# Prompt attention by pairs of heads, with transposed probabilities multiplied into transposed outputs

## What is computed

```python
q = rms_norm((h @ w_q).reshape(B, T, 16, 64), q_norm)
for each block of 128 queries, over keys up to its end:
    s = einsum('bqhd,bkhd->bhqk', q, k) * 64 ** -0.5
    s = s + f_query - f_key          # running sums of log forget gates
    s = where(key <= query, s, -1e30)
    p = softmax(s)
    o = einsum('bhqk,bkhd->bqhd', p, v)
y = concat(o) @ w_o
```

## Time and profile before

| | us |
|---|---|
| median of 3 runs | 1319.04 |
| lowest and highest | 1318.5, 1324.37 |
| the profiled execution, its own time | 1321.06 |
| its span, first to last instruction | 1319.4 |
| PE busy in the span | 1120.7 |
| DVE, ACT, POOL busy | 449.5, 254.2, 131.6 |

### The profile page before, as it was taken

One profiled execution on the slowest core, in us unless ns is written; L12 is line 12 of the kernel. 1 busy time (PEld: TensorE's weight loads), 2 busy tenths in 40 slices (PEclk: granted clock), 3 DMA queues, 4 the chain that ended last, 5 costly groups with the idle time before them and its releaser, 6 DMA issues.

```text
span 1319.4 us, 18188 instructions
## 1 busy us (share of the span) xinstructions
PE 1120.7 (85%) x6958; PEld 633.6 (48%) x6958; DVE 449.5 (34%) x1065; ACT 254.2 (19%) x580; POOL 131.6 (10%) x228
## 2 busy tenths in 40 slices
PE   3996799999997399999977888769966999999980
PEld 0553444444554244445546767545444544445540
DVE  3555601111111540642166676321366011101115
ACT  2232011111111311111123444211120111111111
POOL 4100100000000200000112000210000000000003
PEclk9897799999999699999998999889987999999995
DMA  9998799999999568633424000845034899999976
GB/s 354 380 396 337 256 365 412 413 414 401 400 387 391 201 255 291 260 133 112 150 65 116 0 0 0 245 96 188 16 136 168 326 414 411 411 401 398 387 301 211
DMA packets 66301, 349.55 MB, mean 265 GB/s; under 512 B 6873, under 2 KB 8449, under 8 KB 53378
## 3 DMA queue, kind: packets, MB, share of 16 engines
q1 hardware_dynamic: 46944, 289.72, 56.0%
q0 software_dynamic: 15360, 52.91, 12.7%
q10 hardware_dynamic: 3938, 6.09, 1.3%
HBM read 325.44 MB, written 27.20 MB: 267 GB/s over the span
## 4 chain that ended last, share of the span: by engine, by line
PE 67%; DMA 12%; DVE 11%; issue 5%; ACT 2%; ACTq 2%; POOL 1%; SPq 0%; DVEq 0%; POOLq 0%
PE pb L1151 15%; PE pb L918 11%; PE pb L908 11%; PE pb L954 5%; PE pb L962 5%; DMA h<-h_d,idx 4%; DMA ring<-in_ada_w_dram 3%; PE pb L779 3%; PE pb L1253 2%; PE pb L901 2%; DMA hT_raw<-f_d 2%; PE pb L826 2%; DVE ring L2346 1%; PE pb L1230 1%; PE pb L1102 1%
## 5 line engine op out<-in xcount | busy, mean ns | idle before, releaser
L1151 PE MATMUL pb<-ring,hT_raw 128*128 128x512 f32 x512 | 231.4, 607 | 3.7 <-DVE ring L2207 1.9
L918 PE MATMUL pb<-ring,h 128*64 128x256 f32 (+1 forms) x2176 | 186.5, 345 | 0.0
L1151 PEld LDWEIGHTS pb<-ring,hT_raw 128*128 128x128 f32 x512 | 97.3, 194 | 122.8 <-issue 122.1
L908 PE MATMUL pb<-ring,h 128*128 128x512 f32 x320 | 147.9, 613 | 2.0 <-DVE h L2027 2.0
L918 PEld LDWEIGHTS pb<-ring,h 128*64 128x64 f32 (+1 forms) x2176 | 116.5, 127 | 61.1 <-issue 15.6
L2114 DVE COPY hT_raw<-pb 64x512 f32<-64x512 f32 (+1 forms) x26 | 18.0, 693 | 253.5 <-PE pb L962 146.8
L908 PEld LDWEIGHTS pb<-ring,h 128*128 128x128 f32 x320 | 60.6, 197 | 72.0 <-issue 72.0
L779 PE MATMUL pb<-ring,cT 128*32 128x512 f32 (+1 forms) x576 | 60.1, 556 | 26.2 <-DMA ring<-in_ada_w_dram 26.2
L962 PE MATMUL pb<-ring,hT_raw 128*64 128x512 f32 x352 | 80.1, 597 | 1.0 <-issue 1.0
L954 PE MATMUL pb<-ring,hT_raw 128*128 128x512 f32 x160 | 71.3, 599 | 0.0
L671 POOL DMA_DIRECT2D ys_d<-hT_raw x32 | 18.0, 564 | 489.0 <-DVE hT_raw L2114 397.3
(11 more groups left out here) (333 smaller groups left out, 1329.2 us busy)
## 6 DMA issues: line engine op xcount, KB each, us to landing
ring<-in_w_down_dram SPq DMA_DIRECT2D x32, 2048.0 KB, 14.0
ring<-in_w_gate_dram SPq DMA_DIRECT2D x32, 2048.0 KB, 11.5
ring<-in_w_up_dram SPq DMA_DIRECT2D x32, 2048.0 KB, 12.9
ring<-in_ada_w_dram SPq DMA_DIRECT2D x24, 2048.0 KB, 10.1
ring<-in_kv_ada_w_dram SPq DMA_DIRECT2D x4, 2048.0 KB, 10.0
ring<-in_w_kvf_dram SPq DMA_DIRECT2D x4, 2048.0 KB, 18.5
ys_d<-hT_raw POOLq DMA_DIRECT2D x10, 512.0 KB, 7.8
h_d<-h ACTq DMA_DIRECT2D x8, 512.0 KB, 7.4
```

What stands on the lines that cost most here:

```text
L908: last = T.matmul(bank[:, :], xgT[:, par, k, :], w[:, k * DE:(k + 1) * DE], start=(k == 0), stop=(k == KC - 1))
L918: last = T.matmul(bank[n * a:n * a + n, c0:c0 + cols], xgT[:, par, k, t0:t0 + n], w[:, k * DE + cols * a:k * DE + cols * a + cols], start= ...
L1151: last = T.matmul(bank[:, :], hT[:, k, col[t]:col[t] + P], w[:, k * 512:(k + 1) * 512], start=(k == 0), stop=(k == KC - 1))
```

## The change

The loop is written out, without registers, as 32 steps m: eight pairs times four query tiles in the order 0, 3, 1, 2, each step with both heads of the pair.

- Scores: the masks go first into two PSUM banks, one per head; then each head's product runs on its own 64 rows of the array (`tile_position=(64 * s, 0)`), both heads in turn, with `qT` itself as the weights. `qz` and its copies go: the scale of the scores is multiplied into the query norm's gain once.
- The bias is read from `nfb` in place; POOL's copies go. POOL multiplies the probabilities by the inverse sums instead (`at_sc`), 128 x w per head and step, ahead of the transposes.
- Transposed tiles are copied so that tiles 0 and 1, and tiles 2 and 3, lie side by side (`PTa`, `PTb`). DVE copies tiles 0, 1 and 2, ACT tile 3. The value product has a 64-column block of values as the weights and up to 256 columns of transposed probabilities moving; head s writes rows 64 s to 64 s + 63 of a bank. So outputs come out transposed, two halves a pair, and ACT copies them to `oT`.
- The output projection reads `oT`; only the sample tile is still transposed, from `oo_s`. The output weights are loaded with rows in plain order.
- DVE prepares the sample group's queries after its second add instead of before the loop; DVE, not POOL, waits for the bias loads. The output weights' load waits for the last add, `load_values(1)` for the last scores, behind POOL's own steps.
- Layer 1's first expert loads go out as down, up, gate; up now waits for the end of the output projection too, as `oT` lies in its slot.

```diff
+    TURNS = (0, 3, 1, 2)
...
+    READY = [max(TURNS.index(2 * a), TURNS.index(2 * a + 1)) for a in range(2)]
...
-    o_v = w_o[0].rearrange("(p k) n -> p k n", k=KC)
+    o_v = w_o[0].rearrange("(k p) n -> p k n", p=P)
...
-                    elif kind == "g":
+                    elif kind != "d":
                         sp.wait_ge(o_done, 2 * NT)
...
-                for kind in (("d", "g", "u"), ("u", "d", "g"))[layer]:
+                for kind in (("d", "g", "u"), ("d", "u", "g"))[layer]:
...
-            sp.wait_ge(at_o, TP * NH + 1)
+            sp.wait_ge(at_add, 2 * STEPS)
...
+            for m in range(STEPS):
+                b = TURNS[m % TP]
                 for s in range(2):
-                    pool.wait_ge(at_add, 2 * TP * j + TP * (s - 1))
-                    g.tensor_copy(nfh[:, s, :], nfb[:, bass.ds(2 * j + s, 1), :, :].rearrange(
-                        "p o t k -> p (o t k)")).then_inc(at_nf, 1)
-            pool.wait_ge(at_o, TP * NH + 1)
+                    pool.wait_ge(at_rinv, m + 1)
+                    g.tensor_scalar(Sq[b][s], Sq[b][s], rs[:, 2 * b + s, 1:2], None, ALU.mult).then_inc(at_sc, 1)
+            pool.wait_ge(at_s, STEPS)
             load_values(1)
...
+            def masks(m):
+                if m >= 2:
+                    pe.wait_ge(at_add, 2 * m - 2)
+                b = TURNS[m % TP]
+                for s in range(2):
+                    last = T.matmul(pb[2 * (m % 2) + s][:, b * P:(b + 1) * P], identb[:, :], causal[:, :],
+                                    start=True, stop=False)
+                last.then_inc(at_c, 1)
+
+            def scores(m):
+                j, b = m // TP, TURNS[m % TP]
+                pe.wait_ge(at_c, m + 1)
+                for s in range(2 if b else 0):
+                    q = slice(HD * s, HD * s + HD)
+                    T.matmul(pb[2 * (m % 2) + s][:, 0:b * P], qT[q, j, b * P:(b + 1) * P], kT[q, j, 0:b * P],
+                             start=False, stop=False, tile_position=(HD * s, 0))
+                for s in range(2):
+                    q = slice(HD * s, HD * s + HD)
+                    last = T.matmul(pb[2 * (m % 2) + s][:, b * P:(b + 1) * P], qT[q, j, b * P:(b + 1) * P],
+                                    kT[q, j, b * P:(b + 1) * P], start=False, stop=True, tile_position=(HD * s, 0))
+                last.then_inc(at_s, 1)
+
+            def turn(m):
+                b = TURNS[m % TP]
+                pj, last_b = (m - 1) // TP, TURNS[(m - 1) % TP]
+                for s in range(2):
+                    pe.wait_ge(at_sc, 2 * m + s + 1)
+                    if m and last_b == TP - 1:
+                        pe.wait_ge(at_pa, 2 * pj + s + 1)
+                    elif m:
+                        pe.wait_ge(at_pt, 2 * (pj * (TP - 1) + DVE_TURNS.index(last_b)) + s + 1)
                     for c in range(b + 1):
+                        last = T.transpose(pb[4 + s][:, c * P:(c + 1) * P], Sq[b][s][:, c * P:(c + 1) * P], ident[:, :])
                     last.then_inc(at_t, 1)
...
+            def values(j, half):
...
+                for c in range(2 * half + 2):
+                    lone = c == 2 * half + 1
+                    for s in range(2):
...
+                        last = T.matmul(pb[6 + half][HD * s:HD * s + HD, (P if lone else 0):2 * P],
+                                        vv[:, c, (2 * j + s) * HD:(2 * j + s + 1) * HD], p,
+                                        start=(c == 0), stop=lone, tile_position=(0, HD * s))
+                last.then_inc(at_pv, 1)
...
+            for m in range(STEPS):
+                if m + 3 < STEPS:
+                    scores(m + 3)
+                turn(m)
+                for half in range(2):
+                    j, at = divmod(m - 1, TP)
+                    if m and at == READY[half]:
+                        values(j, half)
+                if m + 4 < STEPS:
+                    masks(m + 4)
+            values(NPAIR - 1, 1)
...
-            transposes(oo, 5, lambda t: pe.wait_ge(sa_o, 8) if t == TS else None, by_stride)
+            transposes(oo_s, 5, lambda t: pe.wait_ge(sa_o, 8), lambda src, t, k: src[:, k * P:(k + 1) * P], [TS])
...
+            def out(j, half):
+                act.wait_ge(at_pv, 2 * j + half + 1)
+                A.activation(oT[:, j, 2 * P * half:2 * P * half + 2 * P], pb[6 + half][:, 0:2 * P], ACT.Copy).then_inc(at_o, 1)
+
+            def copy_p(j):
+                if j:
+                    act.wait_ge(at_pv, 2 * j)
+                for s in range(2):
+                    act.wait_ge(at_t, 2 * (j * TP + TURNS.index(TP - 1)) + s + 1)
+                    A.activation(PTb[:, s, :, P:2 * P], pb[4 + s][:, :].rearrange("p (c t) -> p c t", c=TP),
+                                 ACT.Copy).then_inc(at_pa, 1)
...
+            for m in range(STEPS):
+                if m + 2 < STEPS:
+                    expo(m + 2)
+                for half in range(2):
+                    j, at = divmod(m - 2, TP)
+                    if m > 1 and at == READY[half]:
+                        out(j, half)
+                if TURNS[m % TP] == TP - 1:
+                    copy_p(m // TP)
...
+            def add(m):
+                j, b = m // TP, TURNS[m % TP]
+                w = (b + 1) * P
+                for s in range(2):
+                    if m >= TP:
+                        dve.wait_ge(at_t, 2 * (m - TP) + s + 1)
+                    dve.wait_ge(at_s, m + 1)
...
+                    V.tensor_tensor_reduce(out=Sq[b][s], in0=pb[2 * (m % 2) + s][:, 0:w], in1=bias, scale=1.0,
                                            scalar=-3e38, op0=ALU.add, op1=ALU.max,
...
+                dve.wait_ge(at_add, 2 * m + 2)
+                fq, top = Fs[:, b, 2 * j:2 * j + 2], mx[:, 2 * b:2 * b + 2, :]
+                tt(top[:, :, 1], top[:, :, 0], fq, ALU.add)
+                V.tensor_tensor(top[:, :, 2], fq, top[:, :, 1], ALU.subtract).then_inc(at_nb, 1)
...
+            dve.wait_ge(nfb_loaded, 2 * 16 * TP)
+            add(0)
+            add(1)
+            sample_queries()
+            inverse(0)
+            for m in range(STEPS):
+                if m + 2 < STEPS:
+                    add(m + 2)
+                if m + 1 < STEPS:
+                    inverse(m + 1)
+                if TURNS[m % TP] < TP - 1:
+                    copy_p(m)
```

More of the change, by code:

```diff
@@ L1245, in turn @@
                     last.then_inc(at_t, 1)
-                def values(n):
-                    s, b = divmod(n, TP)
-                    pe.wait_ge(at_pt, NB * j + n + 1)
-                    pe.wait_ge(at_o, NB * j + max(n, 1))
-                    for c in range(b + 1):
-                        last = T.matmul(pb[6 + n % 2][:, 0:HD], PT[:, n % 2, c * P:(c + 1) * P],
-                                        vv[:, c, bass.ds(j * 2 * HD + s * HD, HD)], start=(c == 0), stop=(c == b))
-                    last.then_inc(at_pv, 1)
@@ new lines, in _ @@
+            masks(0)
+            masks(1)
+            scores(0)
+            scores(1)
+            masks(2)
+            scores(2)
+            masks(3)
+            for m in range(STEPS):
[8 more added lines that the diff above has]
+                    masks(m + 4)
@@ new lines, in _ @@
+            expo(0)
+            expo(1)
+            for m in range(STEPS):
[7 more added lines that the diff above has]
+                    copy_p(m // TP)
+            for m in range(STEPS, STEPS + 2):
+                for half in range(2):
+                    j, at = divmod(m - 2, TP)
+                    if at == READY[half]:
+                        out(j, half)
```

194 lines of the change are left out of this document (73 added, 121 removed).

## The result

The changed kernel takes **1278.19 us** (median of 4 runs, 1275.87 to 1279.22), beside 1321.7 for the kernel before on the same chip: a ratio of 0.9647, 95% interval 0.9605 to 0.9689. The forecast of 1269 was 9 us too low, and 1278 lies inside its range. The profiled execution took 1279.22 us, its span is 1277.5.

The account below looks back on a forecast made before the run. The order of waits, not bytes or one full engine, was taken to bound prompt attention. Terms of -40 (stage), -5 (sample group) and -5 (transposed outputs) sum to -50 us: 1271 against the profile, 1269 as median; range 1255 to 1296.

Parts of the forecast that it names:

- The pair: Prompt attention loop: one pair of heads every 10.5 us, 9.75 from waits plus 0.75 for hops and collisions; bounds 9.3 and 13.2.
- POOL's price: POOL's eight multiplications by 1/sum in the loop: priced from its copy, up to twice that, 3.6 to 7.2 us a pair, hidden.
- The cover goes at about three times the copy's price: Loop: POOL's multiplications stay hidden beside DVE and ACT until they cost about three times its copy's 0.61 us at 512 columns.
- So ACT's order, not a full engine, sets 9.75: Loop: ACT's sequence of exponentials, last pair's output and tile 3's copies delays DVE and sets 9.75 us a pair.
- PE's 8.6: PE's work in the loop: values 2.2, scores 3.3, transposes 2.2 and masks 0.9 us, together 8.6 a pair.
- Rival 1: Loop on PE: halves don't overlap, or each tile shape change costs; 13.2 us a pair, 1288 us in all; chance 0.2.
- Rival 2: Loop: POOL and DVE hold each other off, slowing DVE's small operations; 13.2 us a pair, about 1288 us; chance 0.1.
- Rival 3: Loop: TensorE's clock stays at 1.2 GHz, PE takes 18.4 us a pair, slower at 1328 us; chance 0.06.
- The stage: Prompt attention up to the sample group's first transposes: ends at 785.0 instead of 824.9, 40 us less.
- Sample group: Group behind the loop: earlier weight and value loads, then its own arithmetic, save 5 us; bounds 2 and 7.
- Transposed outputs: Before the output projection: only the sample tile is still transposed, done in 1.7 us, saving 5 us.
- Layer 1's weights: Expert loads reordered to down, up, gate: later starts are covered by fifty us, so nil; otherwise the price of one load.

Follow-up runs that it names:

- e5: The changed kernel with POOL copying each score tile onto itself instead of multiplying it by 1/sum (division left out): 1267.03 us, ratio 0.9576.
- e1: The changed kernel without POOL's multiplications, PE's transposes waiting for the exponentials instead (probabilities left unnormalised): 1268.77 us, ratio 0.9585.
- e7: The changed kernel with ACT instead of POOL multiplying the second head of tiles 2 and 3, nothing left out: 1269.72 us, ratio 0.9588.
- e10: The changed kernel with POOL multiplying one head by constant 1.0, the other by a two-operand operation repeating the inverse-sum column: 1271.54 us, one run.
- e9: e7 with the next step's masks right behind the transposes, ahead of the value passes: 1267.18 us, ratio 0.9555.
- e3: The changed kernel with DVE instead of POOL multiplying tiles 0 and 1 by the inverse: 1277.4 us, ratio 0.964.

## Why the prediction was right, and where it was not

The sign, the size and most of the sum held. Against the forecast's -50 us the profiled span shrank by 41.9.

- **The pair** was forecast at 10.5 and is 10.13, but not for the reason given; that the numbers are close is in part luck, as the 0.75 us allowed for hops and collisions covered a price that the sum didn't have. The step that failed is POOL's price: "I take its price, since both read and write one tile, and allow twice that: 3.6 to 7.2 us a pair, hidden". It measured 8.7 us, above the upper bound. The copy's price itself was right (615 ns in e5) and hidden, as said; a multiplication isn't a copy on this engine. "The cover goes at about three times the copy's price" was too late as well: it went at 2.5 times, since two of the dearest operations (3.1 us) stand in one round with 7.0 us of PE's and DVE's work.
- **"So ACT's order, not a full engine, sets 9.75"** failed too. Beneath POOL lies PE at 9.40 (e1, e5, e7). In the changed kernel ACT's path is nearly level with the short round: its copies of tile 3 end at 734.14, and tile 1's transposes, which wait for them, begin at 734.17. ACT's path is real, and e10 shows it, but it comes to some 9.1 by what e10 leaves after the hold, an estimate that no run tests.
- **PE's 8.6** measured 9.41 a pair in e7. From the starts in its timeline: values 2.47 (2.2), scores 2.99 (3.3), transposes 2.59 (2.2), masks 1.36 (0.9). Two terms were put at nothing in that sum. Twelve changes of shape at 0.08 us (e7 against e9) make some 1.0, and four times a pair the scores wait for the masks right ahead of them, 0.14 us more than a change, some 0.6 in all; both are estimates from the rows of e7 and e9. Less than said were the scores and the mask passes themselves. The overlap of the row halves was right: four score passes of 384 columns take 0.92 us, where one after another, at the forecast's two cycles a column, they would take 1.28.
- **Rival 1** fell as a whole: 13.2 a pair didn't come. The Trainium skill's rule that a change of tiling mode drains TensorE (TensorEngine Tiling (Array Packing), Key Properties) agrees with the starts in e7 and e9, which have a change 0.08 us dearer than no change. The 0.07 worked out from the earlier trace rows was near that; that PE's 9.5 with it stands so close to a measured 9.40 is luck in part, as the wait for the masks was not in it and the scores were priced too high. It was set aside because 9.5 lay under the 9.75 of the waits; without POOL's price it would have been the bound.
- **Rival 2** is there in part. DVE's two small operations behind an add average 245 and 176 ns instead of 160. The largest such hold in a pair of the changed kernel stands in DVE's timeline:

```profile
740.91 0.58 DVE L1929 TENSOR_TENSOR bands<-bands 128x2 f32<-128x2 f32 x1
...
805.27 0.19 DVE L2457 TENSOR_TENSOR hT_raw<-hT_raw,smask 128x32 f32<-128x32 f32 x1 [1.20 <-DMA hT_raw<-f_d]
...
873.62 0.70 DVE L1900 TENSOR_TENSOR pb<-pb,mod 128x512 f32<-128x512 f32 x1 [14.98 <-DMA mod<-ada_d]
```

- **Rival 3** fell: the granted clock is 0.53 from 699 to 715 and 1.00 from there to 775; it falls to a mean of 0.81 only at the end, where PE waits for POOL.
- **The stage.** From the last query copies to the sample group it shrank from 129.8 to 94.0 us, by 35.8 where 40 was forecast. The start was 1.0 later and the seven pairs together 1.0 shorter than said (10.36 on average with the first, at half clock), but the end, "PE is done about 8.0 after its t = 0", took 12.2: the last three tiles queue on POOL (from 779.86, 7.35 us), and the last sixteen value passes then run at half clock (granted 0.50 from 789.4 to 792.5), 3.20 us instead of 1.73.
- **Sample group**, -5: its outputs come 64.4 us behind the group's first transposes (856.96) instead of 69.8, so -5.4. The second block's wait for loads fell from 9.48 us to 1.20, the row at 805.27 above.
- **Transposed outputs**, -5: from the sample outputs to the output projection it took 7.4 us and takes 1.9, -5.5.
- **Layer 1's weights**, nil: right for the weights, the gate matmul still comes behind the gathered rows. Missed was what the removed transposes had covered: the gate rows' loads, now issued from 0.5 us ahead of the 2 MB down load to 2.2 us behind it, hold DVE's first add (the row at 873.62) and PE for 2.27 us. The output projection begins 43.25 us earlier (902.11 to 858.86), the span is only 41.9 shorter.
- **Not shown** is how the 5.2 us that a pair lost (15.31 to 10.13) divide among the parts of the change, the fewer value passes, the dropped query and bias copies and the outputs of 256 columns: no run undoes one of them alone.

## What to carry to other kernels

When a change puts an operation on an engine that hasn't done it in the trace, the nearest row of that engine is a bound for the same kind of operation only; take the price at which it would close the loop, and ask whether the unknown could reach it. A round of waits is shortened by splitting a piece that stands in it (e7), not by relieving the engine of pieces that don't (e3). An engine's wait for its own earlier work counts too, and can be covered by putting other work between. And before a stage is taken out, look for the loads that it covered.

## What the runs showed of the hardware that I had not expected

- On POOL at 128 x 512 fp32: copy 615 ns, multiplication by a constant 1490, by a scalar for each partition 1563, by a second operand that repeats one column 1041.
- DVE's small operation of 0.16 to 0.17 us lasted 1.05 us once a pair beside POOL's two-operand multiplication (e10), against 0.58 beside the one-operand form.
- A change of tile shape took PE 0.08 us, and the scores' wait for the masks just ahead of them on PE 0.14 us more than that, four times a pair (e7 against e9).
